# Ending the first query block tile by tile, with the first heads scored inside it

## The chip, the core and the metric

The kernel runs on one core of a Trainium2 chip. A core has TensorE (PE, matrix products into the PSUM banks), VectorE (DVE), ScalarE (ACT) and GpSimd (POOL), and SyncE (SP) that here only issues loads; each runs its own list of instructions in order, and they meet at semaphores. Sixteen DMA engines move data between HBM and SBUF. The metric is the device time of one execution in microseconds.

## What is computed

The reference applies two blocks to 256 tokens of width 2048. The first has a gated MLP branch and a stick-breaking attention branch, each behind an RMS norm. The second has a mixer of a convolution and an mLSTM, a layer norm, and then the part in which the change lies, a feed-forward layer that looks up experts by product keys (`peer_ffn`):

```python
q = (xt @ wq).reshape(-1, PEER_HEADS, 2, PEER_HALF)
s = jnp.einsum('thpc,hpnc->thpn', q, keys)
sv, si = lax.top_k(s, PEER_TOPK)
cand = (sv[:, :, 0, :, None] + sv[:, :, 1, None, :]).reshape(-1, PEER_HEADS, PEER_TOPK * PEER_TOPK)
cid = (si[:, :, 0, :, None] * N_KEYS + si[:, :, 1, None, :]).reshape(-1, PEER_HEADS, PEER_TOPK * PEER_TOPK)
top_s, top_j = lax.top_k(cand, PEER_TOPK)
eid = jnp.take_along_axis(cid, top_j, axis=-1)
gate = jax.nn.softmax(top_s.astype(jnp.float32), axis=-1)
ue = jnp.take(u, eid, axis=0)
act = jax.nn.gelu(jnp.einsum('thkd,td->thk', ue, xt).astype(jnp.float32), approximate=False)
ve = jnp.take(v, eid, axis=0)
return jnp.einsum('thk,thkd->td', (gate * act).astype(xt.dtype), ve)
```

There are 8 heads, 128 keys in each half, 16 picks for each head and token, and 16384 experts. A layer norm ends the block.

## The kernel before

The 256 tokens are two tiles of 128. Every weight matrix is streamed in chunks of 128 rows and 1024 columns (512 KB). SP loads a chunk into one of four raw slots; ACT rounds it to its high part (`round_hi`, L1198), DVE subtracts that to get the low part (`split_lo`, L1584), and both parts lie in one of four split slots. PE multiplies a chunk with both tiles: 12 matmuls of 512 columns, three pairs of high and low parts for two tiles and two banks (`multiply`, L751). A slot is free again when PE has counted the chunk's products. A block is 16 chunks here. ACT and DVE run four chunks ahead of PE: their step k of a block works on chunk k + 4, so the last four steps prepare the first chunks of the next block.

The eight PSUM banks are two halves, A and B, of four banks each. A block's products fill one half, banks 0 and 1 for tile 0, banks 2 and 3 for tile 1, while the other half serves transposes and small products. `UNITS` lists who uses which half in which order, and `is_free`, `is_filled` and `is_emptied` wait on counters that follow from that list.

The order on each engine is written out by hand. `block_of` takes a table `at` of jobs: a job listed at k runs after step k of the block, on that engine, in its order. With `by_tile`, which the last blocks of the attention and of the mixer (`att_out1`, `mix_out1`) use, PE takes the last four chunks first for tile 0 and then for tile 1 (L763), and counts `tile_products` when tile 0 is through.

Around the change the order is this. `peer_q0` (half A) gives the queries of heads 0 to 3 for all tokens, `peer_q1` (half B) those of heads 4 to 7. ACT copies `peer_q0` whole out of PSUM (`take`, L1224). After chunk 0 of `peer_q1` PE turns the first four head halves of tile 0 (`turn_first`, L789), after chunk 1 it scores them against the turned keys (`score_first`, L1082), after chunk 2 it turns the others of that block (`turn_others`, L1091), and after chunk 4 it scores these (`score(0)`, L1104). ACT copies each result.

DVE chooses experts by groups of two heads of one tile. `choosing(n)` gives ten jobs: wait for the scores; the best eight and the next eight of 128 (L2089 to L2101); the sums of pairs (L2126, L2127); the best eight and the next eight of 256 pairs; the exponents' arguments (L2137); a look-up for either key (L2146 to L2152); and the expert numbers `eid` (L2156). Groups 0 and 1 are chosen during `peer_q1`, with the jobs between the splits; the second group's look-ups run after the last split of the block.

Then the gathers: POOL fetches one row of `peer_u` for each token and pick (1 MB for 128 tokens, L676), 256 in all. Rows 0 to 5 go as soon as group 0's numbers are there, into space that is free by then; row 6 and later wait for the last product of `peer_q1`, since their space holds the split weights and the block's input. When `peer_q1` is through, ACT copies its queries and then h of tile 0 into PSUM (L1459), and DVE starts the dot products, one for each gathered row (`dot_row`, L2224). Further groups are chosen between these rows, and the products with the gathered and dense parts of `peer_v` follow.

Of the kernel before, what the change touches and what calls it, by code (L numbers as in the profile page):

```python
# [138 lines left out]
def one_hot_row(m):  # L139
# [35 lines left out]
    + [("keysT", B, False), ("xT_peer0", B, False), ("peer_q0", A, True)] + [(f"xT_peer{i}", B, False) for i in range(1, len(LN_PARTS))]  # L175
    + [("peer_q1", B, True), ("pqT_first", A, False), ("scores_first", A, False), ("pqT0", A, False), ("scores0", A, False), ("pqT1", A, False), ("scores1", A, False),
       ("picks0", B, False), ("keys1", B, False), ("picks1", A, False)]
# [35 lines left out]
def build(nc, x, norm_g, a_w_in, a_v_norm_g, a_w_s, a_b_s, a_w_out, b_w_in, b_w_out, final_g, ln_in_g_2, ln_in_b_2,  # L213
# [6 lines left out]
    with ctx:  # L220
# [202 lines left out]
        def sem(name):  # L423
            return ctx.enter_context(nc.semaphore(name))
# [31 lines left out]
        wg_padded = sem("wg_padded")  # L456
        tile_products = sem("tile_products")
        h_added = sem("h_added")
        gate_abs = sem("gate_abs")
# [66 lines left out]
        def halves(unit):  # L526
            return NTH[unit][0]
# [208 lines left out]
        def _(pe):  # L736
            mm = nc.tensor.matmul

            def multiply(half, c, xts, at, by_tile=False):
# [17 lines left out]
                for t in range(TILES):  # L757
                    for k in range(together, kts):
                        pe.wait_ge(split_done, c + (k + 1))
                        xt, kk, s = xts[k // KT], k % KT, k % SPLIT_SLOTS  # L760
                        for xp, wp in ((0, 0), (0, 1), (1, 0)):
                            for n in range(2):
                                last = mm(ps[half][:, 2 * t + n, :], xt[:, xp, kk, t * P:(t + 1) * P],  # L763
                                          w_split[:, s, wp, n * BANK:(n + 1) * BANK],
                                          start=False, stop=(k == kts - 1 and xp == 1))
                        if t + 1 == TILES:
                            last.then_inc(products, 1)
                        elif k + 1 == kts:
                            last.then_inc(tile_products, 1)
# [7 lines left out]
            def block_of(unit, xts, at={}, by_tile=False):  # L777
                is_free(pe, unit)
                multiply(halves(unit), FIRST[unit], xts, at, by_tile)
# [160 lines left out]

            def normed_block(unit, name, count, at):

# [6 lines left out]
                for k, more in at.items():  # L949
                    jobs.setdefault(k, []).extend(more)  # L950
                block_of(unit, (xT2,), jobs)

# [118 lines left out]
            def turn_first():  # L1071

                is_emptied(pe, "peer_q0")
                turn("pqT_first", [(pq_tok[0][:, 0, k * P:(k + 1) * P], P) for k in range(FIRST_KEYS)])

            def score_first():

                emptied("pqT_first", "keysT")()
                is_free(pe, "scores_first")
                hf = halves("scores_first")  # L1080
                for n in range(FIRST_KEYS):
                    last = mm(by_128[hf][:, n, :], pqT[0][:, n, 0:P], keysT[:, n, :], start=True, stop=True)  # L1082
                filled_by(last, "scores_first")

# [25 lines left out]
            turn_keys()  # L1110
            normed_block("peer_q0", "xT_peer", 6 + len(LN_PARTS), {})
            block_of("peer_q1", (xT2,), {0: [turn_first], 1: [score_first], 2: [turn_others], 4: [score(0)]})
            turn_pq(1)()
# [72 lines left out]
        def _(act):  # L1186
# [242 lines left out]
            parts[0]()  # L1429
            block_of("peer_q0", at={0: [parts[1]], 1: [parts[2]], 4: [parts[3]], 7: [parts[4]]})  # L1430
            take("peer_q0", pq_tok[0][:, :, :], by_tile[A])

            def scores_out(u):
                return copy_out(f"scores{u}", scores[u][:, :, :, :].rearrange("p t n k -> p (t n k)"))

            FIRST_KEYS = 2 * GROUP_HEADS

            def first_turned():
                is_filled(act, "pqT_first")
                take("pqT_first", pqT[0][:, 0:FIRST_KEYS, 0:P], by_128[A][:, 0:FIRST_KEYS, :])  # L1440

# [5 lines left out]
            def first_scored():  # L1447
                is_filled(act, "scores_first")
                take("scores_first", scores[0][:, 0, 0:FIRST_KEYS, :], by_128[A][:, 0:FIRST_KEYS, :])

# [4 lines left out]

            block_of("peer_q1", at={0: [first_turned], 1: [first_scored], 2: [others_turned], 4: [others_scored]}, last=True)
            take("peer_q1", pq_tok[1][:, :, :], by_tile[B])
# [115 lines left out]
        def _(dve):  # L1573
# [506 lines left out]
            for job in (norm[0], norm[1], lo_of[0], lambda: last_splits("mix_out1", 1), norm[2], lo_of[1], norm[3]):  # L2080
                job()
            block_of("peer_q0", at={1: [lo_of[2]], 2: [norm[4]], 4: [lo_of[3]], 7: [lo_of[4]]})


# [25 lines left out]
            def choosing(n):  # L2110
# [4 lines left out]
                def scores_there():  # L2115
                    is_emptied(dve, f"scores{u}" if n else "scores_first")

# [122 lines left out]
            def keys_of(t):  # L2240
# [5 lines left out]
            first, second = choosing(0), choosing(1)  # L2246
            block_of("peer_q1", at={0: [halving_by], 1: first[0:2], 2: first[2:3], 3: first[3:5], 4: first[5:7],
                                    5: first[7:8], 6: first[8:], 7: second[0:2], 8: second[2:3], 9: second[3:5],
                                    10: second[5:7], 11: second[7:]}, last=True)
            ALL = TILES * PICKS  # L2250
# [127 lines left out]
```

## Time and profile before

| | |
|---|---|
| median of 3 runs | 2961.72 us (2961.16 to 2962.39) |
| profiled execution | 2965.63 us, its span 2963.9 us |
| busy in the span: PE, DVE, ACT, POOL | 79%, 69%, 38%, 28% |
| mean granted TensorE clock | 0.884 of full |
| DMA | 792.14 MB, mean 267 GB/s |
| largest shares of the chain that ended last | PE L751 53%, gathered `v_rows` 10%, DVE dots L2224 9% |

The profiler records one execution, and its times are in microseconds from the start of its span. The time of that execution is the 2965.63 us; the span leaves out what lies before its first and after its last record. The shares are means over stages of different kinds: the weight stream, in which PE is always busy, ends at about 1771 us, and after it there are the gathers, with PE idle. A releaser in brackets is the instruction that ended an idle time, found from the semaphores.

### The profile page before, as it was taken

The numbers are of one execution on the slowest core, as the hardware profiler recorded it, in microseconds if no ns is written. First come the engines' busy times: TensorE is split into PE (matmuls) and PEld (weight loads), VectorE is DVE, ScalarE is ACT, GpSimd is POOL, SyncE is SP. The second block draws the span as 40 slices with busy tenths as digits, with TensorE's granted clock in tenths as the row PEclk, the third lists the DMA queues.
The fourth block names the chain that finished last, engine by engine and source line by source line (L and its number), as shares of the span: only waits on it lengthen the run. The fifth ranks groups of instructions, "written<-read, shape, count | busy, mean of one in ns | idle before, by whom it ended". The sixth has DMA issues, their size and how long they took to land.

```text
span 2963.9 us, 29163 instructions
## 1 busy us (share of the span) xinstructions
PE 2339.0 (79%) x10495; PEld 1848.7 (62%) x10495; DVE 2035.8 (69%) x2513; ACT 1120.3 (38%) x1257; POOL 819.3 (28%) x646
## 2 busy tenths in 40 slices
PE   9999999999999999999999990000022249998997
PEld 7888888888888888888888770000011136555654
DVE  5456554554544565745665678999999888887888
ACT  5444344444444554444344442211222244222222
POOL 1000000000000000000000017888887875554553
PEclk9999999999999999999999995555555559999998
DMA  8666556666666546555566469999999967999997
GB/s 281 207 187 193 168 179 189 183 194 188 184 191 185 169 137 206 159 175 170 171 186 224 160 219 403 415 416 417 417 404 397 416 284 297 408 408 388 408 407 301
DMA packets 165304, 792.14 MB, mean 267 GB/s; under 512 B 20188, under 2 KB 20240, under 8 KB 131248
## 3 DMA queue, kind: packets, MB, share of 16 engines
q1 hardware_dynamic: 105344, 390.12, 41.0%
q0 software_dynamic: 59824, 400.23, 33.4%
q8 instruction: 83, 1.36, 0.2%
q14 instruction: 53, 0.43, 0.0%
HBM read 788.17 MB, written 2.10 MB: 267 GB/s over the span
## 4 chain that ended last, share of the span: by engine, by line
PE 58%; DVE 18%; DMA 13%; issue 6%; POOL 3%; ACT 1%; POOLq 0%; SPq 0%; DVEq 0%; ACTq 0%
PE banks L751 53%; DMA v_rows<-in_peer_v_rest,eid 10%; DVE ring L2224 9%; DVE banks L2298 3%; DMA ring<-in_peer_u,eid 3%; POOL ring L676 2%; PE banks L789 1%; PE banks L1135 1%; DVE v_split L2309 1%; POOL v_rows L718 1%; POOL ring L685 1%; PE banks L763 1%; DVE onehots L2203 0%; DVE cand L2127 0%; PE banks L838 0%
## 5 line engine op out<-in xcount | busy, mean ns | idle before, releaser
L751 PE MATMUL banks<-w_split,xT 128*128 128x512 f32 x7008 | 1611.6, 391 | 6.4 <-DVE xT L1631 5.4
L751 PEld LDWEIGHTS banks<-w_split,xT 128*128 128x128 f32 x7008 | 1314.2, 188 | 279.9 <-DVE xT L1631 6.1
L1584 DVE TENSOR_TENSOR w_split<-w_raw,w_split 128x1024 fp32r<-128x1024 f32 x592 | 722.3, 1224 | 733.2 <-ACT w_split L1198 732.0
L1198 ACT ACTIVATE w_split<-w_raw 128x1024 fp32r<-128x1024 f32 x592 | 626.5, 1059 | 913.4 <-PE banks L751 874.5
L2224 DVE CUSTOM_DVE_ANT_0 ring<-ring,banks 128x2048 f32<-128x2048 f32 x194 | 438.5, 2284 | 48.0 <-DMA ring<-in_peer_u,eid 44.1
L2298 DVE SCALAR_TENSOR_TENSOR banks<-v_rows,wgt,banks 128x896 f32<-128x896 f32 x254 | 292.9, 1153 | 67.8 <-DMA v_rows<-in_peer_v_rest,eid 66.5
L676 POOL DMA_INDIRECT ring<-in_peer_u,eid x256 | 245.4, 959 | 257.9 <-DVE eid L2156 157.8
L718 POOL DMA_INDIRECT v_rows<-in_peer_v_rest,eid x256 | 245.6, 959 | 233.2 <-DVE banks L2298 196.7
L1166 PE MATMUL banks<-v_raw,wT 128*128 128x512 f32 (+1 forms) x1024 | 298.9, 435 | 0.7 <-ACT wT L1494 0.7
L1135 PE MATMUL banks<-onehots 128*128 128x128 f32 x512 | 103.7, 370 | 245.1 <-DVE onehots L2203 233.8
L611 POOL DMA_DIRECT2D row_a<-in_final_g x1 | 0.5, 534 | 1063.3 <-DVE ao L1846 1063.3
L685 POOL TENSOR_TENSOR ring<-ring,h 128x2048 f32<-128x2048 f32 x62 | 280.3, 4521 | 39.3 <-DMA ring<-in_peer_u,eid 38.4
L1467 ACT ACTIVATE ring<-ring 128x2048 f32<-128x2048 f32 x62 | 118.4, 1910 | 406.3 <-POOL ring L685 406.3
L1166 PEld LDWEIGHTS banks<-v_raw,wT 128*128 128x128 f32 x1024 | 174.6, 191 | 135.3 <-issue 123.4
L1121 PE MATMUL banks<-ident,pick_keys 128*128 128x128 f32 x4 | 1.3, 428 | 325.3 <-DVE wgt L2232 325.3
L1135 PEld LDWEIGHTS banks<-onehots 128*128 128x128 f32 x512 | 90.4, 267 | 258.6 <-DVE onehots L2203 243.0
L1160 PE MATMUL banks<-v_split,w_x 128*128 128x512 f32 x768 | 224.9, 424 | 8.4 <-DVE w_x L2306 8.4
L1121 PEld LDWEIGHTS banks<-ident,pick_keys 128*128 128x128 f32 x4 | 0.7, 216 | 325.4 <-issue 325.4
L1160 PEld LDWEIGHTS banks<-v_split,w_x 128*128 128x128 f32 x768 | 123.0, 190 | 58.0 <-DVE v_split L2309 24.4
L1548 ACT ACTIVATE w_x<-wT 128x256 fp32r<-128x256 f32 x128 | 53.2, 416 | 269.8 <-PE banks L1160 269.8
L1550 ACT ACTIVATE v_split<-v_raw 128x512 fp32r<-128x512 f32 x128 | 80.4, 628 | 69.7 <-DMA v_raw<-in_peer_v_dense 67.9
L611 POOL DMA_DIRECT2D row_a<-in_ln_g x1 | 0.5, 531 | 338.6 <-DVE xT L1631 338.6
(322 smaller groups left out, 1341.3 us busy)
## 6 DMA issues: line engine op xcount, KB each, us to landing
w_raw<-in_a_w_in SPq DMA_DIRECT2D x192, 512.0 KB, 3.6
v_raw<-in_peer_v_dense SPq DMA_DIRECT2D x128, 576.0 KB, 7.9
w_raw<-in_b_w_in SPq DMA_DIRECT2D x128, 512.0 KB, 3.5
w_raw<-in_w_in SPq DMA_DIRECT2D x112, 512.0 KB, 3.6
w_raw<-in_a_w_out SPq DMA_DIRECT2D x64, 512.0 KB, 4.3
w_raw<-in_b_w_out SPq DMA_DIRECT2D x32, 512.0 KB, 3.9
w_raw<-in_w_out SPq DMA_DIRECT2D x32, 512.0 KB, 4.5
w_raw<-in_peer_wq SPq DMA_DIRECT2D x32, 512.0 KB, 3.7
```

Of the source, the lines that this page charges most:

```text
L676: nc.gpsimd.indirect_dma_start(out=ring[s][:, :], out_offset=None, in_=peer_u_2[0], in_offset=bass.IndirectOffsetOnAxis(ap=eid[:, r:r + 1] ...
L685: nc.gpsimd.tensor_tensor(ring[s][:, :], ring[s][:, :], h[:, r // PICKS, :], ALU.mult)\
L718: nc.gpsimd.indirect_dma_start(out=v_rows[r % V_SLOTS][:, :], out_offset=None, in_=peer_v_rest[0], in_offset=bass.IndirectOffsetOnAxis(ap= ...
L751: last = mm(ps[half][:, 2 * t + n, :], xt[:, xp, kk, tok], w_split[:, s, wp, n * BANK:(n + 1) * BANK], start=(k == 0 and xp == 0 and wp == ...
L1135: last = mm(by_128[B][:, m % 2 * SCATTER + n, :], onehot_b[s][:, n, :], onehot_a[s][:, n, :], start=True, stop=True)
L1160: return mm(v_banks[t][0], w_x[u][:, wp, 1 - t, :], v_split[u][:, vp, :], start=first and wp + vp == 0, stop=last and vp == 1)
L1166: mm(v_banks[t][1 + n][:, 0:width], wT[:, 1 - t, c, :], v_raw[s][:, lo:lo + width], start=first, stop=last)
L1198: fn(w_split[:, k % SPLIT_SLOTS, 0, :], w_raw[:, k % RAW_SLOTS, :], ACT.Copy).then_inc(hi_done, 1)
L1467: fn(ring[s][:, :], ring[s][:, :], ACT.Copy, accum_out=wgt[:, r:r + 1]).then_inc(rows_summed, 1)
L1584: v.tensor_tensor(w_split[:, s, 1, :], w_raw[:, k % RAW_SLOTS, :], w_split[:, s, 0, :].bitcast(F32), ALU.subtract).then_inc(split_done, 1)
L2224: v.tensor_tensor_reduce(out=ring[s][:, :], in0=ring[s][:, :], in1=flat[1 - r // PICKS], scale=1.0, scalar=0.0, op0=ALU.mult, op1=ALU.add, ...
L2298: v.scalar_tensor_tensor(out=v_sum, in0=v_rows[r % V_SLOTS][:, :], scalar=wgt[:, r:r + 1], in1=v_sum if m else h[:, t, V_DENSE:], op0=ALU. ...
```

## The change

In `peer_q0` the last four chunks run tile by tile. When tile 0 is through, ACT copies its queries alone (`first_queries`) while PE goes on with tile 1. After tile 1's chunk 12 PE turns the first four head halves into the bank that tile 0 has left, and after its chunk 13 it scores them into tile 0's other bank; ACT copies both between its roundings. Two new semaphores, `first_taken` and `first_filled`, order these steps, and the units `pqT_first` and `scores_first` leave the list. The other turns and scores of the block move two steps up in `peer_q1`, to chunks 0 and 2. On DVE the first group's first two jobs move into `peer_q0` at step 13, and all later jobs of both groups move two steps up: those that stood at steps 2 to 11 of `peer_q1` now stand at 0 to 9.

```diff
--- before.py
+++ after.py
@@ -173,7 +173,7 @@
     + [("mix_ch", A, True), ("mix_cB", B, True), ("zT", A, False), ("mix_o", A, True), ("cBT", B, False)]
     + [("mix_out0", B, True), ("ymT", A, False), ("mix_out1", A, True)]
     + [("keysT", B, False), ("xT_peer0", B, False), ("peer_q0", A, True)] + [(f"xT_peer{i}", B, False) for i in range(1, len(LN_PARTS))]
-    + [("peer_q1", B, True), ("pqT_first", A, False), ("scores_first", A, False), ("pqT0", A, False), ("scores0", A, False), ("pqT1", A, False), ("scores1", A, False),
+    + [("peer_q1", B, True), ("pqT0", A, False), ("scores0", A, False), ("pqT1", A, False), ("scores1", A, False),
        ("picks0", B, False), ("keys1", B, False), ("picks1", A, False)]
 )
 
@@ -455,6 +455,8 @@
         wg_done = sem("wg_done")
         wg_padded = sem("wg_padded")
         tile_products = sem("tile_products")
+        first_taken = sem("first_taken")
+        first_filled = sem("first_filled")
         h_added = sem("h_added")
         gate_abs = sem("gate_abs")
         gate_ln = sem("gate_ln")
@@ -765,6 +767,8 @@
                                           start=False, stop=(k == kts - 1 and xp == 1))
                         if t + 1 == TILES:
                             last.then_inc(products, 1)
+                            for job in at.get(k, ()):
+                                job()
                         elif k + 1 == kts:
                             last.then_inc(tile_products, 1)
 
@@ -938,7 +942,7 @@
             block_of("att_out1", (xT1,), by_tile=True)
 
 
-            def normed_block(unit, name, count, at):
+            def normed_block(unit, name, count, at, by_tile=False):
 
                 parts = [turn_part(name, q, h, count + q, tiles) for q, tiles in enumerate(LN_PARTS)]
                 there = [emptied(f"{name}{q}") for q in range(len(LN_PARTS))]
@@ -948,7 +952,7 @@
                         11: [there[4]]}
                 for k, more in at.items():
                     jobs.setdefault(k, []).extend(more)
-                block_of(unit, (xT2,), jobs)
+                block_of(unit, (xT2,), jobs, by_tile)
 
             def turn_heads(unit, src, after):
                 def job():
@@ -1070,17 +1074,18 @@
 
             def turn_first():
 
-                is_emptied(pe, "peer_q0")
-                turn("pqT_first", [(pq_tok[0][:, 0, k * P:(k + 1) * P], P) for k in range(FIRST_KEYS)])
+                pe.wait_ge(first_taken, 1)
+                for k in range(FIRST_KEYS):
+                    last = nc.tensor.transpose(by_128[A][:, k, :], pq_tok[0][:, 0, k * P:(k + 1) * P], ident[:, :])
+                last.then_inc(first_filled, 1)
 
             def score_first():
 
-                emptied("pqT_first", "keysT")()
-                is_free(pe, "scores_first")
-                hf = halves("scores_first")
+                emptied("keysT")()
+                pe.wait_ge(first_taken, 2)
                 for n in range(FIRST_KEYS):
-                    last = mm(by_128[hf][:, n, :], pqT[0][:, n, 0:P], keysT[:, n, :], start=True, stop=True)
-                filled_by(last, "scores_first")
+                    last = mm(by_128[A][:, FIRST_KEYS + n, :], pqT[0][:, n, 0:P], keysT[:, n, :], start=True, stop=True)
+                last.then_inc(first_filled, 1)
 
             def turn_others():
 
@@ -1108,8 +1113,8 @@
 
             keep_awake("keysT", LN2_FILL)
             turn_keys()
-            normed_block("peer_q0", "xT_peer", 6 + len(LN_PARTS), {})
-            block_of("peer_q1", (xT2,), {0: [turn_first], 1: [score_first], 2: [turn_others], 4: [score(0)]})
+            normed_block("peer_q0", "xT_peer", 6 + len(LN_PARTS), {12: [turn_first], 13: [score_first]}, by_tile=True)
+            block_of("peer_q1", (xT2,), {0: [turn_others], 2: [score(0)]})
             turn_pq(1)()
             score(1)()
 
@@ -1427,17 +1432,18 @@
 
             parts = normed_parts("xT_peer")
             parts[0]()
-            block_of("peer_q0", at={0: [parts[1]], 1: [parts[2]], 4: [parts[3]], 7: [parts[4]]})
-            take("peer_q0", pq_tok[0][:, :, :], by_tile[A])
-
             def scores_out(u):
                 return copy_out(f"scores{u}", scores[u][:, :, :, :].rearrange("p t n k -> p (t n k)"))
 
             FIRST_KEYS = 2 * GROUP_HEADS
 
+            def first_queries():
+                act.wait_ge(tile_products, TILES + 1)
+                fn(pq_tok[0][:, 0, :], by_tile[A][:, 0, :], ACT.Copy).then_inc(first_taken, 1)
+
             def first_turned():
-                is_filled(act, "pqT_first")
-                take("pqT_first", pqT[0][:, 0:FIRST_KEYS, 0:P], by_128[A][:, 0:FIRST_KEYS, :])
+                act.wait_ge(first_filled, 1)
+                fn(pqT[0][:, 0:FIRST_KEYS, 0:P], by_128[A][:, 0:FIRST_KEYS, :], ACT.Copy).then_inc(first_taken, 1)
 
             def others_turned():
                 is_filled(act, "pqT0")
@@ -1445,15 +1451,19 @@
                 take("pqT0", pqT[0][:, :, P:], by_tok[A][:, :, P:])
 
             def first_scored():
-                is_filled(act, "scores_first")
-                take("scores_first", scores[0][:, 0, 0:FIRST_KEYS, :], by_128[A][:, 0:FIRST_KEYS, :])
+                act.wait_ge(first_filled, 2)
+                fn(scores[0][:, 0, 0:FIRST_KEYS, :], by_128[A][:, FIRST_KEYS:2 * FIRST_KEYS, :], ACT.Copy)\
+                    .then_inc(first_taken, 1)
 
             def others_scored():
                 is_filled(act, "scores0")
                 take("scores0", scores[0][:, :, :, :].rearrange("p t n k -> p (t n) k")[:, FIRST_KEYS:, :],
                      by_128[A][:, FIRST_KEYS:, :])
 
-            block_of("peer_q1", at={0: [first_turned], 1: [first_scored], 2: [others_turned], 4: [others_scored]}, last=True)
+            block_of("peer_q0", at={0: [parts[1]], 1: [parts[2]], 4: [parts[3]], 7: [parts[4]], 11: [first_queries],
+                                    12: [first_turned], 13: [first_scored]})
+            take("peer_q0", pq_tok[0][:, 1, :], by_tile[A][:, 1, :])
+            block_of("peer_q1", at={0: [others_turned], 2: [others_scored]}, last=True)
             take("peer_q1", pq_tok[1][:, :, :], by_tile[B])
             is_emptied(act, "peer_q1")
             fn(flat[B], h[:, 0, :], ACT.Copy).then_inc(h_copied, 1)
@@ -2079,8 +2089,6 @@
             norm, lo_of = normed_parts("xT_peer", h, row_a, row_b)
             for job in (norm[0], norm[1], lo_of[0], lambda: last_splits("mix_out1", 1), norm[2], lo_of[1], norm[3]):
                 job()
-            block_of("peer_q0", at={1: [lo_of[2]], 2: [norm[4]], 4: [lo_of[3]], 7: [lo_of[4]]})
-
 
             def best16(values, rest, top, where, groups):
 
@@ -2113,7 +2121,10 @@
                 u, part = divmod(q * 2 * GROUP_HEADS, PEER_HEADS)
 
                 def scores_there():
-                    is_emptied(dve, f"scores{u}" if n else "scores_first")
+                    if n:
+                        is_emptied(dve, f"scores{u}")
+                    else:
+                        dve.wait_ge(first_taken, 3)
 
                 if n >= CHOSEN_BEFORE:
                     k = 0 if n <= CHOSEN_EARLY else 1
@@ -2244,9 +2255,11 @@
 
 
             first, second = choosing(0), choosing(1)
-            block_of("peer_q1", at={0: [halving_by], 1: first[0:2], 2: first[2:3], 3: first[3:5], 4: first[5:7],
-                                    5: first[7:8], 6: first[8:], 7: second[0:2], 8: second[2:3], 9: second[3:5],
-                                    10: second[5:7], 11: second[7:]}, last=True)
+            block_of("peer_q0", at={1: [lo_of[2]], 2: [norm[4]], 4: [lo_of[3]], 7: [lo_of[4]], 11: [halving_by],
+                                    13: first[0:2]})
+            block_of("peer_q1", at={0: first[2:3], 1: first[3:5], 2: first[5:7], 3: first[7:8], 4: first[8:],
+                                    5: second[0:2], 6: second[2:3], 7: second[3:5], 8: second[5:7], 9: second[7:]},
+                     last=True)
             ALL = TILES * PICKS
 
             choices = {n: choosing(n) for n in range(CHOSEN_BEFORE, ALL_GROUPS)}
```

## Rows read from the trace of the kernel before

**Rows 1.** The chain of waits across peer_q1's end: start, us, engine and line.
```profile
1765.13 5.98 PE banks L751 x24
1771.13 1.89 ACT pq_tok L1224
1773.04 1.89 ACT banks L1459
1775.05 2.29 DVE ring L2224
```

**Rows 2.** The same chain, earlier: TensorE's pieces, start, us, matmuls.
```profile
1670.72 5.49 PE banks L751 x12
...
1723.57 0.63 PE banks L789 x4
...
1726.96 0.89 PE banks L1082 x8
...
1730.60 1.31 PE banks L1091 x12
...
1737.40 2.68 PE banks L1104 x24
```

**Rows 3.** Timeline: a block's tile-by-tile end, ScalarE's roundings and copies [idle before <-releaser].
```profile
1650.20 11.04 PE L763 MATMUL banks<-w_split,xT 128*128 128x512 f32 x48
...
1717.88 1.06 ACT L1198 ACTIVATE w_split<-w_raw 128x1024 fp32r<-128x1024 f32 x1 [1.66 <-PE banks L751]
...
1720.60 1.06 ACT L1198 ACTIVATE w_split<-w_raw 128x1024 fp32r<-128x1024 f32 x1 [1.66 <-PE banks L751]
...
1728.03 0.58 ACT L1224 ACTIVATE scores_a<-banks 128x512 f32<-128x512 f32 x1
...
1732.44 1.02 ACT L1224 ACTIVATE pqT<-banks 128x1024 f32<-128x1024 f32 x1
```

**Rows 4.** Timeline of VectorE in peer_q1, first instruction of each piece.
```profile
1745.14 0.18 DVE L2146 TENSOR_TENSOR topa<-topj,halving 128x32 uint32<-128x32 uint32 x1
...
1752.89 0.86 DVE L2089 MAX8 sv<-scores_a 128x8 f32<-128x128 f32 x4
...
1757.15 0.87 DVE L2098 MAX8 sv<-left 128x8 f32<-128x128 f32 x4
...
1760.37 0.22 DVE L2126 TENSOR_TENSOR sif<-si,ones 128x64 f32<-128x64 uint32 x1
...
1763.85 1.23 DVE L1584 TENSOR_TENSOR w_split<-w_raw,w_split 128x1024 fp32r<-128x1024 f32 x1
1764.99 0.74 DVE L2098 MAX8 tops<-left 128x8 f32<-128x256 f32 x2
...
1767.94 0.18 DVE L2146 TENSOR_TENSOR topa<-topj,halving 128x32 uint32<-128x32 uint32 x1
...
1773.18 0.19 DVE L2156 SCALAR_TENSOR_TENSOR eid<-pick_keys 128x32 uint32<-128x32 f32 x1
```

**Rows 5.** Timeline of TensorE ahead of peer_q0.
```profile
1668.17 0.63 PE L789 MATMUL banks<-ident,h 128*128 128x128 f32 x4 [2.06 <-ACT keysT L1224]
1670.72 1.65 PE L751 MATMUL banks<-w_split,xT 128*128 128x512 f32 x3 [1.93 <-DVE xT L1631]
```

**Rows 6.** Windows: length, busy PE, PEld, DVE, ACT, POOL; clock, DMA share, GB/s.
```profile
1670.00:1672.00 2.00, 1.28 (x3) 1.09 (x4) 2.00 (x4) 0.00 (x0) 0.00 (x0) 0.50 0.00 0
1676.00:1680.00 4.00, 4.00 (x22) 3.43 (x21) 2.08 (x4) 1.77 (x3) 0.00 (x0) 0.92 0.02 4
1770.00:1772.00 2.00, 1.09 (x5) 0.56 (x3) 1.86 (x5) 0.87 (x1) 0.13 (x1) 1.00 0.36 152
1800.00:1850.00 50.00, 0.00 (x0) 0.00 (x0) 41.63 (x67) 10.01 (x10) 41.94 (x27) 0.50 0.98 399
```

**Rows 7.** Timeline of POOL: the gather of row 6.
```profile
1771.87 1.37 POOL L676 DMA_INDIRECT ring<-in_peer_u,eid  x1 [10.60 <-PE banks L751]
```

**Rows 8.** DMA issues of the page: KB each, median us from issue to landing.
```profile
v_raw<-in_peer_v_dense SPq DMA_DIRECT2D x128, 576.0 KB, 7.9
```

## The prediction

> **What bounds the kernel now.** I read the chain of waits from the end of the first query block to the first dot product, then the timeline of VectorE there, then the windows for the DMA share. Behind VectorE's split of peer_q1's chunk 14 [rows 4] the chain says what ends last: the last two chunks on TensorE, ScalarE's copy of the queries, its copy of h into the banks, and the first ring dot product [rows 1]. From there the gathers fill the DMA engines: share 0.98 at 399 GB/s while TensorE does nothing [rows 6]. The gather of row 6 waits for the last product, 10.60 us long, and starts 0.74 us after it [rows 7]. So both things that run the next stage, VectorE's dots and row 6's gather, start from one event, the end of peer_q1's products at 1771.13. What the change is worth is how far it moves that event. Rows 0 to 5 are gathered before it in both kernels, and nobody uses them before h is copied.
>
> In peer_q1 TensorE is not alone at the limit. A chunk costs it 2.72 us (the two weight roundings at 1717.88 and 1720.60, each released by one finished chunk [rows 3]). VectorE splits a weight chunk and does a piece of choosing in each step, and the steps are 2.95 to 4.62 us long [rows 4], more than a chunk. The splits are four chunks ahead of TensorE at the start, so VectorE eats this lead until, at chunk 14, TensorE waits for it: the split from 1763.85 ends at 1765.08, and the products start at 1765.13 [rows 1, 4].
>
> **The change, part by part.**
>
> *TensorE's own work* stays the same: the same matmuls in another order. The earlier block that already runs its last four chunks tile by tile does 48 matmuls in 11.04 us, 0.23 us each [rows 3], as in the other order, so a chunk of one tile takes 1.36 us, half of 2.72. The first turning (0.63 us) and first scoring (0.89 us) only move ahead of the block's end [rows 2].
>
> *The waits put between tile 1's products.* Tile 0 ends 4 x 1.36 = 5.44 us before the block's old end at 1720.60, at 1715.16. ScalarE copies 128x1024 in about 1.02 us (a copy of that size [rows 3]) while TensorE does tile 1's chunk 12 for 1.36 us: hidden with 0.2 us to spare. The second copy stands behind the rounding of a weight chunk (1.06 us) and takes 0.58 us [rows 3], 1.64 together, under 0.63 us of turning and 1.36 us of chunk 13: 0.3 us to spare. I take nothing. Without the cover they would cost 1.1 and 1.7 us; the bounds are 0 and 2.8. The four stages of weights that are freed late (a slot is now free only after tile 1's product of its chunk) come back every 1.36 us while TensorE works 6.96 us before it needs the first of the next block: 1.06 us of rounding and 1.23 us of split fit.
>
> *When choosing starts.* Products of chunk 13 on tile 1 end at 1715.16 + 1.36 + 0.63 + 1.36 = 1718.51; rounding and splitting weight chunk 1 of peer_q1 take until 1720.9, and the scores are copied by then (turned and scored by 1719.4, copied 0.58 us behind that rounding). So choosing starts near 1720.9.
>
> *VectorE's order, which decides.* Choosing of a group has the pieces first eight (a), next eight (b), sums and first eight of the pairs (c), next eight and exponents (d), first look-up (e), second look-up with the expert numbers (f). Before, the last look-ups of the second group stand behind the split of chunk 15, the last one. After, they stand at step 9 of peer_q1, behind the split of chunk 13 and ahead of the splits of chunks 14 and 15. With the split behind it a piece costs, from start to start: e and f 7.75 with their two splits (1745.14 to 1752.89), a 4.26, b 3.22, c 4.62, d 2.95; a split alone 1.14 (1763.85 to 1764.99); and e and f together without a split 5.43 us (1767.94 to 1773.37, the end of the last row) [rows 4]. VectorE has no idle time within these rows, so they add up.
>
> Early in peer_q1 the new order has slack. From 1720.9, a, the splits of chunks 2 to 4 (about 3.5 us) and b end at 1729.6, and the split of chunk 5 waits for TensorE's chunk 1 and the rounding to 1730.0; then split, c, split and d end at 1737.6. The split of chunk 7 can't start before TensorE has done chunk 3: 1720.60 + 0.63 + 0.89 + 4 x 2.72 + 1.31 (the other turns) + 2.68 (the other scores) [rows 2] = 1736.99, plus 1.06 us of rounding and two handovers of 0.04: 1738.1. From here VectorE has no more pauses:
>
> 1738.1 + 1.14 (split 7) + 7.75 (e, split 8, f, split 9) + 4.26 (a, split 10) + 3.22 (b, split 11) + 4.62 (c, split 12) + 2.95 (d, split 13) = 1762.0, + 5.43 (e and f) = 1767.5, + 1.23 (split 14) = 1768.7.
>
> The same sum without pause from 1720.9 would give 1767.9, the lower bound of this term. TensorE, without waits, is through chunk 12 at 1736.99 + 9 x 2.72 = 1761.5, waits some 0.7 us in all for chunks 12 and 13, finishes 13 at 1764.9 and then has nothing for 3.85 us. From the split of chunk 14 to the end, the chain of before takes 1765.13 to 1771.13 = 6.00 us [rows 1], some 0.5 us over two chunks of 2.72; I give 0.2 us of that to a wait for chunk 15's split, which ends when d's row does, at about 1768.0 [rows 4], just behind chunk 14, and leave 0.3 us as start-up. Now chunk 15 is split by 1769.9, in time: 5.7 us. The end of the products comes at 1768.75 + 5.7 = 1774.45, against 1771.13: **3.3 us later**. The start-up of 0.3 us is the loosest part, so 2.5 to 3.6 without the other unknowns.
>
> *What hangs on it.* Both copies (1.89 us each), the first dot and row 6's gather follow from that end without slack of their own [rows 1, 7], and the DMA engines are full until the gathers are done, so the 3.3 us go through to the end. The earlier expert numbers of group 0 (numbers at 1745.9; before, one split ahead of 1752.89 [rows 4]) let POOL gather rows 0 to 5 some 5.9 us sooner. That is worth nothing: row 6 still waits for the products, and the six rows wait for the first dot.
>
> *Weight loads beside the earlier gathers.* A load on SP's queue waits for the split of four chunks before. Chunk 13's is issued at 1747.1 and must be rounded by 1760.9: 12.7 us to land. Loads of 576 KB beside full gathers later in the kernel land in 7.9 us [rows 8]. Hidden; the price if not is below.
>
> The profiled execution took 2965.63 us; with 3.3 us it would be 2968.9. The median of the runs shown is 2961.72, so I forecast **2965.0 us** (+0.11%).
>
> **The rivals.** A difference of 0.2% is 5.9 us, which is about what a measurement of this kernel can tell from no change.
>
> 1. *The clock falls in the hole.* TensorE idles 3.85 us before chunk 14. Ahead of peer_q0 it idled 2.06 us and, after 0.63 us of turns, 1.93 us more [rows 5]; then the granted clock was 0.50, the half level (1.2 of 2.4 GHz), the next chunk took 5.49 us instead of 2.72 [rows 2], and full clock was back only inside 1676 to 1680 (mean 0.92) [rows 6]. Against it: at 1771, TensorE waited about 2 us for the queries' copy and kept 1.00 [rows 6]. The hole here lies between. One chunk and a little more at the half level costs 2.9 us: 3.3 + 2.9 = 6.2 us, 2967.9, which is slower; both chunks at it 5.3 us, 2970.3; a late fall 1.7 us, 2966.7. It decides from a hole in which the clock falls before chunk 14 starts.
> The Trainium skill, page "TensorE: Matmul & The Clock Gate", section "HAM oscillation — how this bites in real kernels", says that a burst of matmuls that waits for its weights lets the clock fall to half, so that the next burst starts slow. By that rule this rival would be the forecast, 2967.9; the trace agrees where the normed input was waited for (0.50 afterwards) and does not at the 2 us wait after 1771 (1.00), so it stays a rival.
>
> 2. *Choosing is off the path.* If VectorE's pieces were spread well enough, TensorE would never wait in peer_q1: 1720.60 + 0.63 + 0.89 + 1.31 + 2.68 + 16 x 2.72 = 1769.6, which is 1.5 us sooner, 2960.2. For it speaks that choosing starts 8 us earlier; against it that VectorE works in order and the 5.43 us stand ahead of two splits. It would take 4 us less of choosing than the rows show.
>
> 3. *A cover is missing in front of it.* Either the two copies hold TensorE between tile 1's products (up to 2.8 us: 6.1 us, 2967.8), or all six rows (1 MB each, 2.6 us at 399 GB/s, from 1746.8 to 1762.5) go ahead of chunk 13's load: rounded at 1763.6 instead of before 1760.9, 2.7 us, 2967.7.
>
> **How the numbers follow.** The forecast without a fall of the clock 0.55, the first rival 0.30, the second 0.05, the third 0.08, and 0.02 for a gain that no case here explains. Over 0.2% slower are somewhat over half of the first rival (0.17) and of the third (0.05): slower 0.22. Faster 0.02. Same 0.76. The range 2962.5 to 2969.0 leaves out the second rival and the worst of the first.
>
> **What would show it.** After: the first choosing starts near 1721; the first expert numbers near 1746; TensorE's wait for VectorE's w_split ahead of peer_q1's chunk 14 is near 3.9 us, where before hardly any is; VectorE splits chunks 14 and 15 back to back after the second group's expert numbers and then idles over 8 us until the first dot near 1778.4; the last early gather lands some 10 us before row 6's issue near 1775.2. The granted clock after the hole tells the first rival. The prediction is wrong if TensorE doesn't wait there, or waits where the copies of tile 0 are, or if the gather stage isn't moved by the same time.

## The result, and the profile after

The median of 21 runs is 2968.70 us (2964.54 to 2971.17), against 2962.68 us (2958.95 to 2967.90, 21 runs) of the kernel before: ratio 1.0017, 95% interval 1.0011 to 1.0023, which is 5.0 us by the ratio (3.3 to 6.8) and 6.0 us by the medians. The forecast was 2965.0 us, +0.11%, in a range of 2962.5 to 2969.0. The profiled execution took 2969.20 us, its span 2967.5 us.

The chain of waits of the kernel after, across the end of peer_q1 (start, us, engine and line; L1594 is the split, L753 the products, L1229 ScalarE's copy, L793 and L1109 the second query block's turns and scores):

```profile
1767.49 0.20 DVE eid L2167
1767.71 1.24 DVE w_split L1594
...
1769.00 7.35 PE banks L753 x24
1776.37 1.89 ACT pq_tok L1229
...
1778.30 2.78 PE banks L793 x16
1781.10 1.89 ACT pqT L1229
...
1783.12 5.25 PE banks L1109 x32
1788.40 1.89 ACT scores_b L1229
...
1790.57 0.21 DVE banks L2192
...
1791.03 2.29 DVE ring L2235
```

The second group's expert numbers now come first, then the split of chunk 14, then 7.35 us of products where [rows 1] have 5.98. The products end at 1776.37 instead of 1771.13, 5.2 us later. The chain then runs on through the turns and scores of the second query block, which in [rows 1] had no part in it: VectorE's setting-up of constants behind its fourth dot waits for the scores' copy, and the fifth dot starts at 1791.03.

The timeline around tile 1's products and the first group, of the kernel after:

```profile
1715.21 1.03 ACT L1442 ACTIVATE pq_tok<-banks 128x1024 f32<-128x1024 f32 x1 [4.32 <-PE banks L765]
1716.29 0.44 PEld L1079 LDWEIGHTS banks<-ident,pq_tok 128*128 128x128 f32 x4 [0.18 <-ACT pq_tok L1442]
...
1717.60 0.58 ACT L1446 ACTIVATE pqT<-banks 128x512 f32<-128x512 f32 x1
...
1720.69 0.87 DVE L2097 MAX8 sv<-scores_a 128x8 f32<-128x128 f32 x4
...
1745.83 0.19 DVE L2167 SCALAR_TENSOR_TENSOR eid<-pick_keys 128x32 uint32<-128x32 f32 x1
```

The copy of tile 0 is covered (0.18 us of a weight load's idle time, none of TensorE's products), choosing starts at 1720.69 and the first expert numbers at 1745.83. The timeline at the end of the block, of the kernel after (in brackets the idle time before, and what ended it):

```profile
1759.44 5.99 PE L753 MATMUL banks<-w_split,xT 128*128 128x512 f32 x24 [0.56 <-DVE w_split L1594]
...
1765.19 1.06 ACT L1203 ACTIVATE w_split<-w_raw 128x1024 fp32r<-128x1024 f32 x1 [3.77 <-DMA w_raw<-in_peer_wq]
...
1769.00 7.33 PE L753 MATMUL banks<-w_split,xT 128*128 128x512 f32 x24 [3.57 <-DVE w_split L1594]
...
1777.11 0.94 POOL L678 DMA_INDIRECT ring<-in_peer_u,eid  x1 [21.53 <-PE banks L753]
...
1780.19 2.29 DVE L2235 CUSTOM_DVE_ANT_0 ring<-ring,banks 128x2048 f32<-128x2048 f32 x1 [10.12 <-ACT banks L1469]
```

TensorE's hole ahead of chunk 14 is 3.57 us. VectorE, which made it, is idle for 10.12 us afterwards. POOL's wait for row 6 is 21.53 us long (10.60 in [rows 7]): the early rows are fetched sooner, and then nothing is until the products end. The windows show the clock (length, busy PE, PEld, DVE, ACT, POOL, clock, DMA share, GB/s):

```profile
1765.00:1768.00 3.00, 0.42 (x2) 0.00 (x1) 2.79 (x7) 1.06 (x1) 0.00 (x0) 1.00 1.00 423
1768.00:1770.00 2.00, 1.00 (x3) 0.82 (x4) 2.00 (x2) 0.00 (x0) 0.00 (x0) 0.77 0.43 180
1770.00:1772.00 2.00, 2.00 (x6) 1.61 (x5) 0.07 (x1) 0.00 (x0) 0.00 (x0) 0.50 0.03 12
1772.00:1774.00 2.00, 2.00 (x9) 1.57 (x9) 0.00 (x0) 0.00 (x0) 0.00 (x0) 0.88 0.00 0
...
1780.00:1784.00 4.00, 1.94 (x9) 1.57 (x9) 3.81 (x3) 2.04 (x2) 2.21 (x3) 0.50 0.98 393
```

In the hole the granted clock is still 1.00. From chunk 14's first products at 1769.00 it is at its half level (1.2 GHz) up to 1772 and a little beyond; six matmuls fill 2 us. It falls again around the next waits (0.50 from 1780 to 1784), so that the turns take 2.78 us and the scores 5.25 us, where the kernel before has 1.97 and 3.81.

### The profile page after: what moved, and what is told of

Its sections match the earlier page's. It is cut to its first block, busy times and chain, and to the rows that moved or that the text cites. A ratio compares the mean times of both kernels' runs of the same rounds, so it can differ in the third digit from the quotient of the medians.

```text
span 2967.5 us, 29164 instructions
## 1 busy us (share of the span) xinstructions
PE 2343.0 (79%) x10495; PEld 1852.3 (62%) x10495; DVE 2035.4 (69%) x2513; ACT 1120.8 (38%) x1258; POOL 818.2 (28%) x646
## 4 chain that ended last, share of the span: by engine, by line
PE 58%; DVE 18%; DMA 13%; issue 6%; POOL 3%; ACT 1%; POOLq 0%; DVEq 0%; ACTq 0%
PE banks L753 52%; DMA v_rows<-in_peer_v_rest,eid 10%; DVE ring L2235 8%; DVE banks L2311 3%; DMA ring<-in_peer_u,eid 2%; POOL ring L678 2%; PE banks L793 2%; PE banks L1140 1%; PE banks L765 1%; POOL v_rows L720 1%; DVE onehots L2214 1%; DVE v_split L2322 1%; DVE w_split L1594 0%; DVE cand L2138 0%; PE banks L842 0%
## 5 line engine op out<-in xcount | busy, mean ns | idle before, releaser
L753 PE MATMUL banks<-w_split,xT 128*128 128x512 f32 x6960 | 1602.7, 391 | 9.9 <-DVE xT L1641 5.3
L753 PEld LDWEIGHTS banks<-w_split,xT 128*128 128x128 f32 x6960 | 1306.9, 188 | 282.6 <-DVE xT L1641 6.1
L1594 DVE TENSOR_TENSOR w_split<-w_raw,w_split 128x1024 fp32r<-128x1024 f32 x592 | 721.9, 1224 | 731.4 <-ACT w_split L1203 730.1
```

The lines of the kernel that those rows point to most:

```text
L753: last = mm(ps[half][:, 2 * t + n, :], xt[:, xp, kk, tok], w_split[:, s, wp, n * BANK:(n + 1) * BANK], start=(k == 0 and xp == 0 and wp == ...
L1594: v.tensor_tensor(w_split[:, s, 1, :], w_raw[:, k % RAW_SLOTS, :], w_split[:, s, 0, :].bitcast(F32), ALU.subtract).then_inc(split_done, 1)
```

## The experiments

Two theories were set against each other. The first: VectorE's order puts 5.4 us of look-ups ahead of the last two splits; that makes the hole, and the clock falls behind the hole. The second: the tile-by-tile end, or the earlier gathers beside the last weight loads, cost the time.

The traces are compared by one interval, because the profiled executions reach this stage up to 2.9 us apart: from the start of the rounding of peer_q0's last chunk on ScalarE (1709.71 in the kernel before, 1709.83 after) to ScalarE's copy of peer_q1, which starts when the products have ended (1771.13 and 1776.37). One execution of each kernel was profiled, so the interval is that of one execution; the ratio is from all runs.

| kernel | interval, us | against before, us | ratio to before, 95% interval |
|---|---|---|---|
| before | 61.42 | | |
| after | 66.54 | +5.1 | 1.0017 (1.0011 to 1.0023) |
| look-ups behind the last split | 61.10 | -0.3 | 0.9992 (0.9983 to 1.0001) |
| 24 products in the hole | 66.48 | +5.1 | 1.0016 (1.0007 to 1.0025) |
| tile by tile, choosing at the old steps | 63.26 | +1.8 | 1.0007 (0.9998 to 1.0016) |
| look-ups cut in two by a split | 63.36 | +1.9 | 1.0009 (1.0000 to 1.0018) |
| first one, gathers held | 61.07 | -0.4 | 0.9998 (0.9989 to 1.0007) |
| pieces spread | 60.98 | -0.4 | 0.9998 (0.9989 to 1.0007) |
| before, with look-ups ahead | 68.46 | +7.0 | 1.0026 (1.0015 to 1.0036) |
| 14 products in the hole | 64.98 | +3.6 | 1.0013 (1.0004 to 1.0022) |

**Look-ups behind the last split.**

```diff
-...8: second[5:7], 9: second[7:]},
+...8: second[5:7], 11: second[7:]},
```

> The changed kernel with one edit: VectorE does the second group's look-ups after the split of peer_q1's last chunk (step 11), not at step 9. Theory (VectorE's order makes the hole ahead of chunk 14, and the hole lets the clock fall): the split of chunk 14 follows that of chunk 13, TensorE idles under 1 us in all in peer_q1, both last chunks run at full clock, the products end 5 to 6 us sooner than in the changed kernel, near 1770.5, and the time is 0.7 us under the kernel before (ratio 0.9993 to 1.0001). Rival (the tile-by-tile end, or weight loads beside the earlier gathers, cost the time): the ratio stays at 1.0010 or more. A smaller doubt: chunk 15's load landed late in the changed kernel (rounded from 1765.19 to 1766.25); if it binds once the order is mended, TensorE waits for it by up to 0.6 us.

Median 2961.90 us (11 runs) against 2962.96. The chain of this kernel:

```profile
1756.98 1.24 DVE w_split L1594
...
1758.26 11.46 PE banks L753 x48
...
1769.74 1.89 ACT pq_tok L1229
```

The last four chunks run without a break, 11.46 us for 48 matmuls. Its timeline of VectorE, on the doubt about chunk 15's load:

```profile
1759.93 2.35 DVE L1594 TENSOR_TENSOR w_split<-w_raw,w_split 128x1024 fp32r<-128x1024 f32 x2
...
1765.32 1.23 DVE L1594 TENSOR_TENSOR w_split<-w_raw,w_split 128x1024 fp32r<-128x1024 f32 x1 [3.04 <-ACT w_split L1203]
...
1771.71 0.19 DVE L2167 SCALAR_TENSOR_TENSOR eid<-pick_keys 128x32 uint32<-128x32 f32 x1
...
1773.66 2.29 DVE L2235 CUSTOM_DVE_ANT_0 ring<-ring,banks 128x2048 f32<-128x2048 f32 x1 [1.76 <-ACT banks L1469]
```

The split of chunk 15 waits 3.04 us for a rounding that waits for its load, yet ends at 1766.55, about when TensorE asks for it. The look-ups still end before the first dot, which waits for the copy of h as in the kernel before. With one edit the whole loss is gone; the tile-by-tile end and the earlier gathers are still in this kernel. The products end 0.3 us sooner than in the kernel before, not 0.7, and the ratio 0.9992 is a little under the range expected.

**Look-ups cut in two.**

```diff
-...8: second[5:7], 9: second[7:]},
+...8: second[5:7], 9: second[7:8], 10: second[8:]},
```

> The changed kernel with the second group's first look-up left at step 9 and the second look-up with the expert numbers at step 10, so that the 5.4 us are cut in two by the split of chunk 14. Theory (what counts is how much of VectorE stands ahead of each of the last splits): two holes of about 0.9 and 1.2 us instead of one of 3.6, no fall of the clock, products end near 1773.0, 1.9 us after those of the kernel before, ratio 1.0006 (1.0002 to 1.0010), between the first run and the changed kernel. Rival (any work of look-ups between the splits costs the whole): as the changed kernel, 1.0015 to 1.0021.

Median 2965.11 us against 2962.96. TensorE's timeline:

```profile
1766.04 3.04 PE L753 MATMUL banks<-w_split,xT 128*128 128x512 f32 x12 [0.70 <-DVE w_split L1594]
1770.03 3.01 PE L753 MATMUL banks<-w_split,xT 128*128 128x512 f32 x12 [0.95 <-DVE w_split L1594]
```

Two holes under 1 us each, both chunks at 3.0 us with a granted clock of 1.00 from 1765 to 1774, and 1.9 us in all, the forecast value. Behind the block, against what I expected, the clock did fall: the turns of the second query block take 3.12 us and the scores 6.52. The loss at the end of the products goes by how much of VectorE stands ahead of each split.

**The kernel before, with look-ups ahead.**

```diff
-...8: second[2:3], 9: second[3:5],
-...10: second[5:7], 11: second[7:]}, last=True)
+...8: second[2:3], 9: second[3:7],
+...10: second[7:]}, last=True)
```

> The kernel before, no tile-by-tile end, with the changed kernel's flaw alone as the theory sees it: the second group's next eight and exponents at step 9 of peer_q1 and all its look-ups at step 10, ahead of the split of chunk 15. Theory: TensorE idles near 3.7 us ahead of chunk 15, the products end 5.3 us later (more if the clock falls), ratio 1.0017 (1.0010 to 1.0025). Rival (the loss needs the tile-by-tile end or the earlier gathers): ratio within 0.0005 of 1.

Median 2971.13 us (8 runs) against 2963.37, more than expected. TensorE's timeline:

```profile
1765.72 4.62 PE L751 MATMUL banks<-w_split,xT 128*128 128x512 f32 x12 [2.37 <-DVE w_split L1584]
1772.33 4.60 PE L751 MATMUL banks<-w_split,xT 128*128 128x512 f32 x12 [1.99 <-DVE w_split L1584]
```

I had expected one hole of 3.7 us; the split of chunk 14 is late as well, so there are two, of 2.37 and 1.99 us, and both chunks behind them take 4.6 us where the kernel before has 5.98 us for the two. Holes beyond the old 0.56 us (3.8) and slower chunks (3.2) make the 7.0 us. Neither the tile-by-tile end nor earlier gathers are in this kernel, so the second theory can't account for it.

**Products in the hole.** To part the hole from the clock, TensorE multiplies the identity by itself behind chunk 13, into a bank that is idle there; nobody uses the result.

```diff
+def stay_awake():
+    is_free(pe, "pqT1")
+    for _ in range(24):
+        mm(ps[A][:, SPARE_BANK, 0:P], ident[:, :], ident[:, :], start=True, stop=True)
...
-block_of("peer_q1", (xT2,), {0: [turn_others], 2: [score(0)]})
+block_of("peer_q1", (xT2,), {0: [turn_others], 2: [score(0)], 13: [stay_awake]})
```

> The changed kernel with 24 products of the identity put on TensorE behind peer_q1's chunk 13, into a bank that is idle there, so that it works in most of the 3.6 us hole; the order of VectorE is as in the changed kernel. Theory (hole plus fall of the clock): the split of chunk 14 still ends near 1768.9, the last two chunks take 5.7 us in place of 7.3, and the turns and scores of the second query block 1.97 and 3.81 in place of 2.76 and 5.24; the products end 3.5 us after those of the kernel before, ratio 1.0012 (1.0007 to 1.0016), 2 to 3 us under the changed kernel. Rival (the two chunks were slow for another reason, loads or memory): they stay at 7 us and the ratio at 1.0017 to 1.0021.

Median 2968.90 us against 2962.96, as the kernel after. TensorE's timeline:

```profile
1764.16 5.52 PE L1122 MATMUL banks<-ident 128*128 128x128 f32 x48
1769.43 5.70 PE L753 MATMUL banks<-w_split,xT 128*128 128x512 f32 x24
1777.10 3.02 PE L793 MATMUL banks<-ident,pq_tok 128*128 128x128 f32 x16 [1.97 <-ACT pq_tok L1236]
1782.18 6.62 PE L1109 MATMUL banks<-keysT,pqT 128*128 128x128 f32 x32 [2.06 <-ACT pqT L1236]
```

My count was wrong: one such product shows as two matmuls, and 24 took 5.5 us, more than the hole. The chunks did run in 5.70 us, but started later by what that saved. The turns and scores, expected at 1.97 and 3.81 us, took 3.02 and 6.62: the clock fell behind the next waits all the same. So again with `range(14)`:

> As the run with products of the identity in the hole, but 14 of them, since the 24 took 5.36 us, more than the 3.57 us hole, and so held the chunks up themselves. Theory (hole 3.6 us, fall of the clock 1.6 us, both in the loss): 14 take 3.1 us and end before chunk 14's split; the last two chunks take 5.7 us and not 7.3; the products end 1.6 us sooner than in the changed kernel, ratio 1.0011 (1.0005 to 1.0016). Rival (the last two chunks are slow for another reason): they stay near 7 us, ratio 1.0015 to 1.0020.

Median 2966.70 us against 2963.37. Its timeline, and one of its windows:

```profile
1763.75 3.29 PE L1122 MATMUL banks<-ident 128*128 128x128 f32 x28
1767.46 5.74 PE L753 MATMUL banks<-w_split,xT 128*128 128x512 f32 x24 [0.43 <-DVE w_split L1601]
1775.17 1.97 PE L793 MATMUL banks<-ident,pq_tok 128*128 128x128 f32 x16 [1.97 <-ACT pq_tok L1236]
1779.20 3.81 PE L1109 MATMUL banks<-keysT,pqT 128*128 128x128 f32 x32 [2.06 <-ACT pqT L1236]
```

```profile
1770.00:1773.00 3.00, 3.00 (x15) 2.32 (x13) 0.00 (x0) 0.00 (x0) 0.00 (x0) 1.00 0.00 0
```

Now the clock stays at 1.00 and the two chunks take 5.74 us, while VectorE still holds the chunks up. The interval is 1.6 us shorter than after: that much of the loss was the clock. The turns and scores are as short as in the kernel before, but that can't be put down to the 14 products, since with 24 they were long. In the times the step is 1.0017 to 1.0013, with overlapping intervals; it is the trace that shows it.

**Tile by tile, choosing at the old steps.**

```diff
-...11: [halving_by], 13: first[0:2]})
-block_of("peer_q1", at={0: first[2:3], ... 9: second[7:]}, last=True)
+...11: [halving_by]})
+block_of("peer_q1", at={1: first[0:2], 2: first[2:3], ... 11: second[7:]}, last=True)
```

> Tile-by-tile end, the copies, turns and scores as in the changed kernel, but VectorE chooses at the steps of the kernel before (1 to 11 of peer_q1). Theory (the tile-by-tile end costs nothing, it only makes scores early): products end within 1.5 us of the kernel before, ratio 1.0000 (0.9995 to 1.0005). Rival (waits between tile 1's products, or weights that come free late, cost 2 us or more): ratio 1.0007 or more and TensorE idle between 1715 and 1725.

Median 2964.61 us against 2962.96; the products end 1.8 us later than before, a little outside what I expected. The view of TensorE's waits from 1708 to 1772 has one row (in total, times, longest), and the timelines show where it comes from:

```profile
PE banks L753 <- DVE w_split L1594: 2.2, 3, 1.6
```

```profile
1728.97 1.23 DVE L1594 TENSOR_TENSOR w_split<-w_raw,w_split 128x1024 fp32r<-128x1024 f32 x1 [2.86 <-ACT w_split L1203]
1730.12 0.87 DVE L2097 MAX8 sv<-scores_a 128x8 f32<-128x128 f32 x4
...
1765.86 5.96 PE L753 MATMUL banks<-w_split,xT 128*128 128x512 f32 x24 [1.60 <-DVE w_split L1594]
```

No wait between tile 1's products, so the tile-by-tile end itself costs TensorE nothing. But TensorE's first scores and other turns now stand ahead of chunk 1 of peer_q1 (before, behind chunks 1 and 2), and VectorE waits 2.86 us for that chunk's slot before its first piece: choosing starts 21.5 us after the reference rounding (1708.60 to 1730.12), in the kernel before 19.7 (1709.71 to 1729.37). The 1.9 us arrive at the end as 1.8. The rival's ratio of 1.0007 came out, but not its place; my expectation of no cost was wrong too.

**Gathers held**, on top of the first run:

```diff
 if r % GROUP_PICKS == 0:
     pool.wait_ge(chosen, r // GROUP_PICKS + 1)
+if r == 0:
+    pool.wait_ge(split_done, FIRST["peer_q1"] + 11)
```

> The first run of this study (look-ups behind the last split) with one edit: POOL's first gather also waits for the split of peer_q1's chunk 10, so that the early rows start near 1752 as in the kernel before, not near 1746. Theory (the earlier gathers are worth nothing, and they only crowd the last weight loads): ScalarE's roundings of chunks 14 and 15 no longer wait 5.9 and 3.8 us for their loads but under 2 us, the products end as in the first run or up to 0.6 us sooner, ratio within 0.0008 of its 0.9992. Rival (rows that are there sooner help): slower than the first run by 2 to 5 us, ratio 1.0000 or more.

Median 2962.93 us against 2963.37; the products end as in the first run. Its timeline of POOL and ScalarE:

```profile
1752.61 1.02 POOL L680 DMA_INDIRECT ring<-in_peer_u,eid  x1 [157.64 <-DVE w_split L1596]
...
1764.11 1.06 ACT L1205 ACTIVATE w_split<-w_raw 128x1024 fp32r<-128x1024 f32 x1 [6.58 <-DMA w_raw<-in_peer_wq]
```

The gathers start 5.7 us later than after. Chunk 14's load is no longer late, but chunk 15's still is, by 6.58 us, against what I expected: it is issued behind the start of the held gathers. The ratios 0.9992 and 0.9998 differ by 1.8 us, and each has an interval of 2.7 us to either side, so the times do not settle whether rows that are there sooner are worth anything up to a few microseconds; the trace shows no use of them.

**Pieces spread.**

```diff
-...6: second[2:3], 7: second[3:5], 8: second[5:7], 9: second[7:]},
+...6: second[2:3], 8: second[3:5], 9: second[5:7], 10: second[7:8], 11: second[8:]},
```

> A candidate: the changed kernel with the second group's pieces moved behind the splits that TensorE waits for (sums and pairs at step 8, next eight and exponents at 9, first look-up at 10, second look-up and expert numbers at 11). Theory: TensorE waits for chunk 15 alone, by up to 0.5 us, the products end 0.7 to 1.2 us sooner than in the kernel before, ratio 0.9994 (0.9986 to 1.0001), the least of all runs but not to be told from the first one. Rival (VectorE's last pieces now delay the first dot): the first dot waits for VectorE and not for the copy of h, and the ratio is 1.0000 or more.

Median 2962.86 us against 2963.37. The timelines of TensorE and VectorE:

```profile
1765.06 3.02 PE L753 MATMUL banks<-w_split,xT 128*128 128x512 f32 x12 [0.70 <-DVE w_split L1594]
...
1772.03 2.29 DVE L2235 CUSTOM_DVE_ANT_0 ring<-ring,banks 128x2048 f32<-128x2048 f32 x1 [4.30 <-ACT banks L1469]
```

TensorE waits 0.70 us for chunk 15 alone, and the first dot waits for the copy of h with VectorE idle for 4.30 us. The products end 0.4 us sooner than before, less than the 0.7 expected, and the ratio is not the least of all runs. No version here is told from the kernel before as faster.

## Why the prediction was right in kind and short in size

*No cost of the tile-by-tile end, hidden copies.* Right: TensorE's products wait nowhere there, in the kernel after and in the run with the old steps.

*Start of choosing, first expert numbers.* 1720.9 forecast and 1720.69 measured; 1745.9 and 1745.83.

*VectorE's order.* Right: the split of chunk 14 was to start at 1767.5 and starts at 1767.71, the hole was to be 3.85 us and is 3.57. The first run, the one with the look-ups cut in two and the one on the kernel before show that this order is the cause, and that the loss follows its dose.

*From chunk 14's split to the end, 5.7 us.* This is the term that was mis-sized: the forecast took both chunks at full clock. It took 1769.00 to 1776.37, 7.4 us, because behind the hole the clock was at half. The run with 14 products parts the 5.1 us: 3.6 with the clock kept (forecast 3.3, at most 3.6) and 1.6 for the clock, both rounded up. I had the fall as the first rival, with 0.30. Its 2.9 us took a whole chunk at half clock, as in [rows 2]; in windows of half a microsecond the clock here is 1.00 up to 1769.0, 0.50 from 1769.5 to 1772.0 and 1.00 from 1772.5, inside chunk 14. The 1.7 us that I gave for a late fall come near in size only: the clock fell as chunk 14 started and was back before its end, which none of my three cases had. What I held against the rival was thin: the window of [rows 6] at 1771 ends at 1772, inside the wait that it was to speak for (1771.09 to 1773.06). The Trainium skill, page "TensorE: Matmul & The Clock Gate", section "HAM oscillation — how this bites in real kernels", says that bursts which wait for their data start at half clock. By that rule, the trace agrees: 0.50 behind the hole, and 1.00 where the hole was filled. Behind the holes of 0.70 and 0.95 us the clock stayed at 1.00, so not every wait has that effect.

*The time.* It lies inside the range because the range took in the smaller cases of that rival; the sum alone was short. Of the 3.7 us between 2965.0 and 2968.70, 1.0 is the base (2961.72 from three runs, 2962.68 from 21).

*What hangs on the end.* Right: the products end 5.2 us later, and the time is 5.0 to 6.0 us longer. I had left out that at half clock the scores of the second query block come later too; VectorE's constants wait 1.19 us for their copy, and the fifth dot starts 6.4 us later than before. That this adds to the time is not shown: with the look-ups cut in two that wait is 2.83 us and the fifth dot, counted from the reference rounding, 4.8 us late, but the products end 1.9 us late and the median is 2.2 us longer.

*Earlier gathers.* Loads were hidden, as forecast, but with less to spare than my 7.9 us from [rows 8]: chunk 15's was issued with the split of chunk 11 at 1754.77 and rounded from 1765.19, some 10.4 us later. The six early rows took longer than the 2.6 us each of the third rival: the DMA share is 1.00 from 1765 to 1768 and 0.43 to 1770, so they land some 7 us before row 6's gather at 1777.11, not 10. That rival still did not come about: chunk 13 was rounded at 1753.54, without a wait for its load.

## What to carry to other kernels

When an engine prepares data for another and does work of its own in between, the long pieces belong behind the last preparation, not ahead of it; an early start upstream is lost if the order of the queue spends the lead. Work that nobody waits for (here the second group, first used at row 32) should not stand ahead of a part that sets the next stage's start. And a hole of a few microseconds in TensorE's products is to be priced with the slow matmuls behind it, here 1.6 us on 3.6.

## What was not expected of the hardware

The clock also fell around holes of 2.37 and 1.99 us: in that run the granted clock is 0.66 and 0.65 from 1765 to 1770, 1.00 to 1772, then 0.70 and 0.50 to 1776, and both chunks take 4.6 us. Every kernel here waits 1.97 and 2.06 us behind peer_q1. In the kernel before, these waits left the clock at 1.00:

```profile
1773.06 1.97 PE L789 MATMUL banks<-ident,pq_tok 128*128 128x128 f32 x16 [1.97 <-ACT pq_tok L1224]
1777.08 3.81 PE L1104 MATMUL banks<-keysT,pqT 128*128 128x128 f32 x32 [2.06 <-ACT pqT L1224]
```

So they did with the old steps, with held gathers and with 14 products. In the other six profiles, that of the kernel after among them, the clock was at 0.50 in part or all of the scores, which took 5.24 to 6.62 us: the same wait has either outcome, and no run here shows what decides it.

A load of 512 KB that meets the gathers of POOL takes far longer to land. The DMA issues of the kernel after, from 1751 to 1766 (KB each, median us to landing):

```profile
w_raw<-in_peer_wq SPq DMA_DIRECT2D x2, 512.0 KB, 9.6
```

From 1715 to 1754, ahead of the gathers, the median in the kernel before is 3.5 us. The Trainium skill, page "DMA: Bandwidth & Descriptors", section "Issuing engines are not separate DMA queues", says that transfers of all issuing engines share the same 16 DMA engines and interleave; the trace agrees, with a share of 1.01 between 1760 and 1765 while both were under way.
